# A two-layer decoder step on one core: opening rebuilt without GpSimd, second layer's memory panels moved into the projection, norms on token quarters

## The reference

```python
def _rms_norm(x, g):
    y = xf * lax.rsqrt(jnp.mean(xf * xf, axis=-1, keepdims=True) + EPS) * g
def _mem_kv(mem, g, w_kv, k_g):            # once for each layer, from mem_prompt
    kv = _rms_norm(mem, g) @ w_kv          # (256, 1024) @ (1024, 512)
    return _rms_norm(mk, k_g), mv          # keys normed for each head of 64, values not
...
for i in range(DEPTH):                     # DEPTH = 2
    h = _rms_norm(x, p["norm_mix"][i])
    z = h @ w_in                           # layer 0: q, k, v, qx: 1536 columns
    q = _rope(_rms_norm(q, ...), pos); k = _rope(_rms_norm(k, ...), pos)
    o_self = ...                           # windowed attention, or B * conv3(C * h)
    o_x = _cross_attend(_rms_norm(qx), mem_k[i], mem_v[i])
    x = x + concat(o_self, o_x) @ p["w_out"][i]
    hm = _rms_norm(x, p["norm_mlp"][i])
    x = x + jnp.square(jax.nn.relu(hm @ p["w_up"][i])) @ p["w_down"][i]
```

## Time and profile before

| | |
|---|---|
| median of 3 runs | 1238.41 us (1237.78 to 1238.74) |
| the profiled execution's own time | 1238.45 us |
| its span, first to last instruction | 1236.7 us |
| mean granted TensorE clock | 0.99 |
| PE, DVE, ACT, POOL busy | 97%, 48%, 32%, 17% |

### The profile page before, as it was taken

The page is one execution under the profiler, slowest core; times in us unless marked ns, Lnnn a source line. Parts: engine busy times, 40 slices in busy tenths (PEclk is TensorE's granted clock), DMA queues, the critical chain, the costliest instruction groups (busy, mean ns, idle before and its releaser), DMA issues.

```text
span 1236.7 us, 21836 instructions
## 1 busy us (share of the span) xinstructions
PE 1203.8 (97%) x9436; PEld 1164.1 (94%) x9436; DVE 595.4 (48%) x749; ACT 396.8 (32%) x578; POOL 216.3 (17%) x198
## 2 busy tenths in 40 slices
PE   4899899999999999999999999999999999999998
PEld 4899656999999999999999999999999999999998
DVE  7899765454333423424456645655342432333331
ACT  7332676324213213313332223323321421321320
POOL 7736644330000000000041212242000000000000
PEclk9999889999999999999999999999999999999999
DMA  7433431322222222221222322221222222122221
GB/s 276 164 107 114 140 116 56 137 103 68 103 75 97 97 75 92 77 102 68 102 75 96 137 69 69 70 103 68 103 79 93 75 98 102 68 102 77 93 95 45
DMA packets 22853, 120.16 MB, mean 97 GB/s; under 512 B 2676, under 2 KB 6644, under 8 KB 9732
## 3 DMA queue, kind: packets, MB, share of 16 engines
q1 hardware_dynamic: 17892, 100.93, 23.5%
q0 software_dynamic: 1632, 10.54, 2.3%
q10 hardware_dynamic: 3264, 7.74, 1.8%
HBM read 111.29 MB, written 5.69 MB: 95 GB/s over the span
## 4 chain that ended last, share of the span: by engine, by line
PE 87%; DVE 8%; POOL 1%; DMA 1%; issue 1%; ACT 1%; ACTq 0%; DVEq 0%; POOLq 0%
PE zps L419 80%; DVE tmp L730 2%; DVE w_lo L705 2%; PE tps L528 2%; PE ops L556 1%; PE ops L588 1%; PE zps L483 1%; DVE act_lo L858 1%; POOL sm L1246 1%; DVE act_lo L745 1%; DMA tmp<-z 1%; DVE z L715 0%; PE ops L572 0%; DVE rstd L722 0%; DVE sm L777 0%
## 5 line engine op out<-in xcount | busy, mean ns | idle before, releaser
L419 PE MATMUL zps<-act_hi,w_hi 128*128 128x272 f32 (+1 forms) x2880 | 608.0, 290 | 2.5 <-DVE w_lo L870 2.2
L419 PE MATMUL zps<-act_hi,w_lo 128*128 128x272 f32 (+1 forms) x2880 | 601.9, 289 | 0.0
L419 PE MATMUL zps<-act_lo,w_hi 128*128 128x272 f32 (+1 forms) x2880 | 600.2, 288 | 0.0
L419 PEld LDWEIGHTS zps<-act_hi,w_hi 128*128 128x128 f32 x2880 | 457.0, 189 | 7.5 <-DVE w_lo L870 2.9
L419 PEld LDWEIGHTS zps<-act_lo,w_hi 128*128 128x128 f32 x2880 | 456.3, 189 | 0.1
L419 PEld LDWEIGHTS zps<-act_hi,w_lo 128*128 128x128 f32 x2880 | 453.3, 189 | 0.0
L705 DVE TENSOR_TENSOR w_lo<-w_stage,w_hi 128x2048 fp32r<-128x2048 f32 x91 | 216.6, 2380 | 127.4 <-ACT w_hi L972 127.3
L972 ACT ACTIVATE w_hi<-w_stage 128x2048 fp32r<-128x2048 f32 (+1 forms) x93 | 175.5, 1888 | 277.1 <-PE zps L419 249.4
L753 DVE TENSOR_TENSOR x_res<-zps,x_res 128x544 f32<-128x544 f32 x80 | 57.9, 724 | 227.1 <-PE zps L419 226.3
L1077 ACT ACTIVATE tmp<-tmp 128x544 f32<-128x544 f32 x64 | 42.3, 661 | 246.9 <-DVE tmp L836 246.9
L836 DVE SCALAR_TENSOR_TENSOR tmp<-zps,rstd 128x544 f32<-128x544 f32 x64 | 46.2, 722 | 152.4 <-PE zps L419 152.4
(11 more groups left out here) (116 smaller groups left out, 530.2 us busy)
## 6 DMA issues: line engine op xcount, KB each, us to landing
w_stage<-wst SPq DMA_DIRECT2D x92, 1024.0 KB, 4.9
kx<-xkT POOLq DMA_DIRECT2D x4, 1024.0 KB, 5.3
vx<-xv POOLq DMA_DIRECT2D x4, 1024.0 KB, 7.0
x_res<-xT ACTq DMA_DIRECT2D x1, 2176.0 KB, 11.0
tmp<-z ACTq DMA_DIRECT2D x32, 68.0 KB, 2.0
yT<-x_res ACTq DMA_DIRECT2D x8, 272.0 KB, 2.0
memx<-memT SPq DMA_DIRECT2D x2, 512.0 KB, 4.7
vb<-swav POOLq DMA_DIRECT2D x1, 1024.0 KB, 7.5
```

Source lines behind the costliest of these rows:

```text
L419: mm = pe.matmul(zps[slot][:, h, 0:n], w_[:, d, k, w:w + 128], r_[:, k, c0 + h * n:c0 + (h + 1) * n], start=(j == 0 and i == 0), stop=(j = ...
```

## The change

Five things are done.

1. **The opening without POOL, chunk by chunk.** The first duo is loaded in two halves and split chunk by chunk (`first_hi`, `first_lo`); panels 0 and 1 run side by side over the chunks (`first_panels`), as soon as chunk 0 is there. DVE squares the memory input (two operations of 1024 columns), and PE adds up over the chunks in 8 accumulating quarter sums after chunk 5. A sqrt on a dummy element loads ACT's table before the data are there. x is loaded in four parts, after the first duo.
2. **The second layer's memory panels inside the projection.** The order of panels is now FRONT, s = 0 to 19: 4 memory panels of layer 0, projection panels i = 0 to 3, 4 memory panels of layer 1, i = 4 to 11. The quads of weights are stored in that order. hi and lo of the second memory input have buffers of their own and are made by ACT and DVE at s = 5 to 7. POOL waits for them (`m_los[1]`) before it loads kt, which takes the memory input's place, and before it rotates; it loads vb only after the rotary.
3. **x's squares.** ACT squares x chunk by chunk behind `norm_hi` (`normed_x`), and PE sums each chunk inside panel s = 4 (`token_squares`); POOL's `sum_squares(2)` goes.
4. **Norms on token quarters.** All sums, of tokens and of heads, are now made in quarters: four matmuls with 32 output columns, each over a quarter of the tokens, into the four partition quarters of `tps` (`quarter_sums`). ACT's root and DVE's reciprocal then have 136 columns instead of 544 (64 instead of 256). Four matmuls of 64 rows bring the result to all partitions and tokens (`spread_quarters`), in the middle of the panel after. DVE copies it out for a token norm, or reads it from PSUM for a head norm. This holds for all norms, in both layers.
5. **Branch hints.** PE's two MLP loops get a hint for the branch at their end.

```diff
-Q_MEM, Q_ATT, Q_OUT0 = 0, 2, 5
+Q_MEM, Q_ATT, Q_OUT0 = (0, 2), (1, 3, 4), 5
...
+        FRONT = [(kind, l, 4 * b + p) for kind, l, b in (("mem", 0, 0), ("att", 0, 0), ("mem", 1, 0), ("att", 0, 1), ("att", 0, 2))
+                 for p in range(4)]
...
-            for d in range(2):
-                sp.dma_start(stage[:, d], wst[d]).then_inc(w_in[d], 16)
+            sp.dma_start(stage[:, 0, 0:4, :], wst[0, :, 0:4, :]).then_inc(ld["w0"], 16)
+            sp.dma_start(stage[:, 0, 4:8, :], wst[0, :, 4:8, :]).then_inc(w_in[0], 16)
+            sp.dma_start(stage[:, 1], wst[1]).then_inc(w_in[1], 16)
...
+            def quarter_sums(kind, src, cols, first=True, last=True):
+
+                w = cols // 4
+                for j in range(4):
+                    mm = pe.matmul(tps[32 * j:32 * j + 32, 0, 0:w], kind, src[:, j * w:(j + 1) * w], start=first, stop=last)
+                return mm
+
+            def spread_quarters(cols):
+
+                w = cols // 4
+                for i in range(2):
+                    for half in range(2):
+                        r = slice(64 * half, 64 * half + 64)
+                        mm = pe.matmul(tps[:, half, i * w:(i + 1) * w], con[r, C_SEL + 128 * i:C_SEL + 128 * (i + 1)],
+                                       tmp[r, 3, 0:w], start=True, stop=True)
+                return mm
...
+            def headspread(n):
+                pe.wait_ge(n_inv, n + 1)
+                spread_quarters(norm_cols(n)).then_inc(n_spread, 1)
+                tfree[0] = (n_out, n + 1)
...
-                with pe.Fori(1, GROUPS) as g:
+                with nc.Fori(1, GROUPS, engines=[mybir.EngineType.PE], hint_back_edge=True) as g:
...
+            def first_panels():
+
+                for k in range(KC):
+                    pe.wait_ge(m_los[0], k + 1)
+                    if k < KC - 1:
+                        pe.wait_ge(w_lo_first, k + 1)
+                    else:
+                        pe.wait_ge(w_los[0], 1)
+                    for p in range(2):
+                        for i, (w_, r_) in enumerate(((w_hi, act_hl[1][0]), (w_hi, act_hl[1][1]), (w_lo, act_hl[1][0]))):
+                            mm = pe.matmul(zps[p][:, 0, 0:NMEM], w_[:, 0, k, p * 128:(p + 1) * 128], r_[:, k, 0:NMEM],
+                                           start=(k == 0 and i == 0), stop=(k == KC - 1 and i == 2))
+                        if k == KC - 1:
+                            mm.then_inc(z_full[p], 1)
+                    if k == 5:
+                        pe.wait_ge(ld["con"], 16)
+                        pe.wait_ge(m_sq, 2)
+                        for c in range(KC):
+                            mm = quarter_sums(token_sum, msq[:, c, :], NMEM, c == 0, c == KC - 1)
+                        mm.then_inc(s_full, 1)
+
+            def token_squares(k, _mm):
+
+                if k == 0:
+                    take(tfree)
+                pe.wait_ge(x_sq, k + 1)
+                mm = quarter_sums(token_sum, (psq, pacc)[k % 2], NT, k == 0, k == KC - 1)
+                mm.then_inc(x_sum if k < KC - 1 else s_full, 1)
+
+            first_panels()
+            colspread(1, NMEM)
+            headsum(front_norm(0))
+            for s in range(2, len(FRONT)):
+                kind, l, i = FRONT[s]
+                q, p = s // 4, s % 4
+                mid = [(colspread, (2, NT))] if s == 5 else []
+                if front_norm(s - 2) is not None:
+                    mid.append((headspread, (front_norm(s - 2),)))
...
+            token_inverse(1, NMEM)
+            token_rstd(1, NMEM)
+            for p in range(2):
+                take_scaled(0, p, mem_z[:, p, :], NMEM)
             split_lo(0, 1)
+            head_inverse(0)
+            for k in range(2):
+                norm_lo(0, k, 0)
+            split_lo(1, 0)
+            head_norm(0)
+            take_scaled(0, 2, mem_z[:, 2, :], NMEM)
+            head_inverse(1)
+            norm_lo(0, 2, 0)
+            head_norm(1)
+            take_scaled(0, 3, mem_z[:, 3, :], NMEM)
+            for k in range(3, KC):
+                norm_lo(0, k, 0)
...
+            def normed_x(k):
+
+                if k % 2 == 0:
+                    act.wait_ge(ld[f"x{k // 2}"], 16)
+                norm_hi(0, k, 0)
+                if k >= 2:
+                    act.wait_ge(x_sum, k - 1)
+                act.activation((psq, pacc)[k % 2][:, :], X[:, k, :], ACT.Square).then_inc(x_sq, 1)
...
+            for s in range(4, len(FRONT)):
+                kind, l, i = FRONT[s]
+                split_next(s // 4, s % 4)
+                if s == 4:
+                    root_tokens(2, NT)
+                if front_norm(s) is not None:
+                    square(front_norm(s))
+                if front_norm(s - 1) is not None:
+                    root_heads(front_norm(s - 1))
+                if s in (5, 6, 7):
+                    for k in range((0, 3, 6)[s - 5], (3, 6, 8)[s - 5]):
+                        memory_hi(1, k)
+                if FRONT[s - 2][0] == "att" and FRONT[s - 2][2] < 8:
+                    swapped(FRONT[s - 2][2])
...
-            pool.wait_ge(ld["x"], 16)
-            sum_squares(2, X, NT, lambda k: None)
-            pool.dma_start(vb[:, :, :], swav).then_inc(ld["vb"], 16)
-            for l in range(2):
-                pool.wait_ge(m_los[l], KC)
+            pool.wait_ge(m_los[1], KC)
             pool.wait_ge(m_hi, 16)
             pool.dma_start(kt[:, :, :, 0:128], swakT).then_inc(ld["kt"], 16)
...
             pool.wait_ge(r_out, 8)
+            full(pool, Q_MEM[1], 3)
+            pool.dma_start(vb[:, :, :], swav).then_inc(ld["vb"], 16)
```

More of the change, by code:

```diff
@@ L151, in build_kernel @@
         z_free = [sem(f"z_free{s}") for s in range(2)]
-        ld = {n: sem("ld_" + n) for n in ("con", "con2", "mem0", "mem1", "x", "rope", "kt", "vb", "kx0", "kx1", "vx0", "vx1")}
-        m_hi, m_full, m_los = sem("m_hi"), sem("m_full"), [sem(f"m_lo{l}") for l in range(2)]
+        ld = {n: sem("ld_" + n) for n in ("con", "con2", "mem0", "mem1", "w0", "x0", "x1", "x2", "x3", "rope", "kt", "vb", "kx0", "kx1", "vx0", "vx1")}
+        warm = sem("warm")
+        m_sq, m_hi, m_los = sem("m_sq"), sem("m_hi"), [sem(f"m_lo{l}") for l in range(2)]
         a_his, a_los = sem("a_his"), sem("a_los")
         sq_acc, pool_ch = sem("sq_acc"), sem("pool_chain")
-        s_full, s_sd, s_rstd = sem("s_full"), sem("s_sd"), sem("s_rstd")
-        n_sq, n_ms, n_sd, n_out = (sem("n_" + s) for s in ("sq", "ms", "sd", "out"))
+        x_sq, x_sum = sem("x_sq"), sem("x_sum")
+        s_full, s_sd, s_inv, s_spread, s_rstd = (sem("s_" + s) for s in ("full", "sd", "inv", "spread", "rstd"))
+        n_sq, n_ms, n_sd, n_inv, n_spread, n_out = (sem("n_" + s) for s in ("sq", "ms", "sd", "inv", "spread", "out"))
         r_sw, r_out = [sem(f"r_sw{i}") for i in range(2)], sem("r_out")
@@ L614, in mlp_group @@
                 for m in range(8):
-                    panel(q + m // 4, m % 4, *act_hl[1 - l], ready=first if m == 0 else None)
+                    panel(q + m // 4, m % 4, *act_hl[1 - l], ready=first if m == 0 else None,
+                          between=midway((colspread, (stat, NT))) if m == 1 and stat else None)
                     if m == 0 and stat:
@@ new lines, in token_squares @@
+            def token_squares(k, _mm):
[13 more added lines that the diff above has]
+                    mid.append((headspread, (front_norm(s - 2),)))
+                if kind == "mem":
+                    hi, lo = (act_hl[1], (mem1_hi, mem1_lo))[l]
+                    panel(q, p, hi, lo, 0, NMEM, ready=(lambda k: (m_los[1], k + 1)) if (l, p) == (1, 0) else None, between=midway(*mid))
+                else:
+                    panel(q, p, *act_hl[0], ready=normed(0) if i == 0 else None, between=token_squares if i == 0 else midway(*mid))
+                if front_norm(s - 1) is not None:
+                    headsum(front_norm(s - 1))
+                if s == 3:
+                    pe.wait_ge(ld["con2"], 16)
+                if FRONT[s - 1][0] == "mem" and FRONT[s - 1][2] >= 2:
+                    turn_memv(2 * FRONT[s - 1][1] + FRONT[s - 1][2] - 2)
+                if (kind, i) == ("att", 10):
@@ L716, in take_scaled, with token_inverse, token_rstd, head_inverse @@
                 else:
[L717 removed]
+                    ins = dve.tensor_tensor(out, zps[p % 2][:, 0, 0:cols], mem_rstd[:, 0:cols], ALU.mult)
                 ins.then_inc(z_free[p % 2], 1)
[L720 removed]
+            def token_inverse(n, cols):
                 dve.wait_ge(s_sd, n)
[L722 removed]
+                dve.reciprocal(tmp[:, 3, 0:cols // 4], tmp[:, 2, 0:cols // 4]).then_inc(s_inv, 1)
+            def token_rstd(n, cols):
+                dve.wait_ge(s_spread, n)
+                dve.tensor_copy(wide(rstd if cols == NT else mem_rstd, cols), tps[:, :, 0:cols // 2]).then_inc(s_rstd, 1)
                 dve.wait_ge(s_rstd, n)
+            def head_inverse(n):
+                cols = norm_cols(n)
+                dve.wait_ge(n_sd, n + 1)
```

(20 more changed lines are left out.)

307 lines of the change are left out of this document (131 added, 176 removed).

## The result

The changed kernel took 1249.58 us (median of 4 runs, 1249.01 to 1250.17), the kernel before 1238.58 beside it: a ratio of 1.0084, 95% interval 1.0069 to 1.0098. It is slower by 0.8%; about 1242 was forecast. The profiled execution took 1250.05 us with a span of 1247.3, which is 10.6 longer than before, and 2.75 us around it (1.75 before). The missing 7.7 us of that execution (1250.05 against 1238.45 + 3.9) are read stage by stage. The other executions have nearly the same span (all four 1247.0 to 1247.3); outside it they have 1.8 to 3.0 us.

The account below looks back on a forecast made before the run. PE, busy 97% of the span, was taken as the bound. Opening +8.3, start of attention -7.0 and later norms +2.6 sum to +3.9 us on a profiled 1238.45: about 1242 us, range 1234 to 1247.

Parts of the forecast that it names:

- Price of a sum: Between PE's panels, a quarter sum takes 0.58 and a spread 0.86 us: +0.52 us for each 544-column norm.
- Rival A: PE's interruptions by sums and spreads are cheap: 1236 us at 0.25 per transition, 1233 with half hidden; chance 0.2.
- Part 1: Start of the kernel: first panel matmul at 9.0 us, 8.2 us earlier; memory squares moved to DVE and PE, +2.3.
- Part 2: Norms on quarters: memory norms +3.1, attention projection's ten +5.2, five later norms +2.6, token_squares +4.6 us.
- Part 3: New PE waits up to the opening's last panel: 9.6 us against 8.3 of old ones, +1.3.
- (a): Panel s=2 waits for split_lo(0,1), now behind token_rstd and two takes: 3.1 us.
- (b): In panel 3 the spread of norm 1 waits for head_inverse(1), behind split_lo(1,0) on DVE: 1.3 us.
- (c): Second layer's memory panels (s=8 to 11): spreads and sums wait while ACT is behind swap issues: 5.2 us (0 to 7).
- rival C: Pauses at s=2, 3 and 8 to 11 put PE at 1.2 GHz: slower yet, 1246 us; chance 0.12.
- Rival B: The ACT waits in s=8 to 11 don't happen, its queue having run ahead: -5.2, 1237 us, no change; chance 0.22.
- Part 4: Start of attention: waits for r_out and qs go, -2.9 and -2.5 us; full clock there, -1.6.
- Part 5: Branch hints on PE's MLP loops: no back edge stalls before, so 0 us, bounds 0 and -0.5.

Follow-up runs that it names:

- b_quarters: The kernel before with all its norms on token quarters and nothing else of the change: 1260.46 us, ratio 1.0182.
- a_swaplate: The changed kernel with four swap issues (rotations 2 and 3) moved from opening steps 8 and 9 to 12 and 13: 1246.99 us, ratio 1.0067.
- a_nohint: The changed kernel without the hint on the back edge of TensorE's two MLP loops: 1247.39 us, ratio 1.0077.
- a_pad: The changed kernel, hint kept, with 28 extra semaphore waits (14 more instructions in the trace) ahead of TensorE's first matmul: 1247.75 us, ratio 1.0077.
- a_xdve: The changed kernel, but VectorE adds the eight squared token chunks and TensorE takes one quarter sum behind panel 4: 1248.67 us, ratio 1.0084.
- a_both: The changed kernel without the hint and with four swap issues moved to steps 12 and 13: 1244.7 us, ratio 1.0055.
- a_both_xdve: The changed kernel without the hint, with four swap issues at steps 12 and 13 and token squares added on VectorE: 1242.67 us, ratio 1.0022.
- b_hint: The kernel before with only the hint on TensorE's two MLP loops added: 1240.77 us, ratio 1.0007.
- b_quarters_hint: The kernel before with all norms on quarters and the hint on TensorE's two MLP loops: 1245.03 us, ratio 1.0064.
- b_tail_hint: b_tail with the first of its three spreads moved to the seventh chunk of panel i=9, and the hint on the MLP loops: 1235.2 us, ratio 0.9963.
- b_tail: The kernel before with only the last three of the opening's ten projection head norms (7 to 9) on quarters: 1234.33 us, ratio 0.9966.

## Why the prediction was wrong

The direction and most terms held; the size did not. 7.7 us were missing, by the panel ends: opening +3.6, attention +0.9, from there to the end +2.3, around the span +0.9.

*Price of a sum*: right (0.57 and 0.86). Rival A is out: 0.25 for each transition would have given 6.2 us back. The Trainium skill (TensorEngine Tiling (Array Packing), Key Properties) says that a change of the tiling mode drains TensorE. That agrees with the insertions, which take 0.35 and 0.41 us more than their streams, though no run shows the drain itself. From the page's speedup table alone the estimate for the pair was 0.68; measured are 1.43.

*Part 1*: the start came at 9.6 instead of 9.0 (before 17.2). The sum of the memory squares gave most of it back: it took 1.1 us (between 16.11 and 17.36, less one record) instead of 1.6.

*Part 2*: right to 0.1 us in b_quarters, with the luck told there. token_squares made panel s=4 10.2 us long instead of 6.0, and its last sum, behind the panel, adds 0.4 to 0.6: the 4.6 forecast.

*Part 3*: (a) was right, with waits of 1.43 and 1.76 us against 3.1 (its terms add up to 3.0). (b) was taken too large, 0.6 us against 1.3. **The step that failed is (c)**, taken as 5.2 for spreads and head sums that wait while ACT is behind its swap issues and POOL's r_out. The mechanism is the one named, and the waits were near the right size: PE lacks 4.6 us in 66.1 to 90.2 (POOL's 3.28 us beside DVE's split is part of it, and was in no term). What the term left out is the clock behind them: 0.14 of 24.1 us is up to another 3.4. Together 8.0, which is 2.8 of the 3.6. The other 0.8 is the balance of what lies ahead of s=8, where the clock behind wait (a) (0.88 over 14 us, up to 1.7 us) is the same omission. a_swaplate took the wait away and both parts went. But the clock's part is not fixed: of the four profiled kernels with a wait of 2.3 us before the spread of s=10, the changed kernel and a_nohint have a granted clock of 0.66 in the ten us from there, a_pad 0.83, and a_xdve 1.00; of the three without the wait (a_swaplate, a_both, a_both_xdve) none has a half-clock stretch there. I had the clock only as rival C, with 0.12, and as an alternative to the forecast; it should have stood in the term, as a range from nothing to the full stretch. Rival B (ACT's queue has run ahead) is out.

*Part 4*: the waits for r_out and qs went; the stage gave 6.1 back of 7.0. That the sum came near is partly luck. The waits were to give 5.4, but PE's idle time in the stage fell by 3.0 only (7.5 to 4.5), as waits for ACT's work took part of their place; the clock was to give 1.6, and the other 3.1 came with it (0.88 to 0.94). The half-clock stretches move with the stage's start. Over the nine kernels with all ten norms on quarters it took 81.2 to 85.5 us (by the table), so no time there can be tested to better than some 2 us.

*Part 5*: **wrong, 2.0 us in the span against a bound of 0.** The reasoning was that no back edge stalls before, so there is nothing to gain; that a hint could cost was not weighed. By a_nohint, b_hint and a_pad it costs where loop and following code happen to lie so; why that place, the profile does not show. The Trainium skill (Runtime: NRT & Kernel Launch, Instruction fetch mechanics) says that a taken branch out of the fetched window stalls. The trace of before has no such stall and b_quarters has two (4.9 and 4.1 us), which begin in the branch; that agrees with the page, and whether it happens changes with edits elsewhere in the program. That the two branches waited for instructions to be fetched no run shows. The two executions of a_nohint some 5 us above the rest need no such stall: their granted clock is 0.987 and 0.986 against 0.990 to 0.992, which is worth some 4 us (an estimate), and a_pad and b_quarters_hint, both hinted, have one such execution each, at 0.987 and 0.986.

The hint also goes with the 0.9 us outside the span, for which the prediction had no term. In 48 executions of seven hinted kernels the time outside the span is 1.75 to 3.0 us, and over 2.2 in 20 of them; in 48 executions of six unhinted ones, and in 65 of the kernel before, it is never over 1.9. All six of a_pad and of b_quarters_hint are among the 20, none of a_xdve and b_tail_hint. So this too hangs on the program; the cause stays open. It is why a_pad, without the pause, is timed no faster than a_nohint.

*The rest*: the later five norms cost 5 x 0.5 as forecast. Of the 2.3 us missing behind the first output panel 2.0 are the pause, and 0.4 a longer wait for POOL in layer 1.

What decided the change as a whole: its opening was rebuilt for a start 7.6 us earlier, and by the prediction's own terms (-8.2, +2.3, +4.6, +1.3) it was worth 0; it came out at 148.2 - 144.5 = 3.7 us worse than the old opening with the same norms (b_quarters). And the quarters pay 0.5 us for each norm while only the last three earn: b_tail pays for three and is 0.3% faster (0.2 to 0.5), 4.5 us where the rival expectation (an unloaded DVE over the whole stretch) had 0 to 2. That the chains of the last norms alone take the idle time out of the attention stage is shown by its profile: PE lacks 4.5 us, as with all ten on quarters. In time the stage is 86.0 us there and 82.8 in the changed kernel; the rest is the clock (0.90 and 0.94), and whether all ten norms have a part in that is not shown.

## What to carry to other kernels

Where TensorE lacks nothing, a shorter chain on another engine is worth something only where a wait ends with it: find those few places and pay the extra matmuls there alone. Price a forecast TensorE wait with the half-clock stretch that may follow it, as a range: the same wait had one in three executions of four here. After any edit of a program with loops, look at the back edges and the loop's end for idle time with no releaser; it can come or go by place alone, and a hint is worth trying both ways. Look also at the time outside the span.

## What the runs showed of the hardware

- Unhinted back edges of one and the same loop: no pause before, 4.9 and 4.1 us in b_quarters, where the two branches took 3.67 and 3.37 us (0.21 to 0.26 everywhere else); with the hint none. The hint in turn: a pause of 1.85 or 1.57 us at the loop's end in one PE program, none in b_hint, b_quarters_hint, b_tail_hint, a_xdve and a_pad (14 more instructions ahead of the loop).
- Outside the span: never over 1.9 us in 113 executions of unhinted kernels, up to 3.0 us in hinted ones.
- A full-width operation of POOL (L1378) took 3.28 us beside DVE's split (L770), and 1.33 us six microseconds later, with DVE idle up to 80.34 us.
- Behind waits of 1.43 and 1.76 us (19.6 to 23.16), of 2.33 us (78.6 to 80.95) and a pause of 4.9 us (462.5 to 467.4), TensorE's records ran at half speed for several us. Behind the 1.85 us pause at 659 they did not (the next records stand 0.25 us apart in pairs, as ahead of it), nor behind a wait of 2.34 us in a_xdve (clock 1.00 in 66 to 88), nor behind the last of b_quarters' waits of 2.15 us (51.0; clock 1.00 in 50 to 60). So the length of a wait alone does not tell.
